# Making a state-space layer's tables and block matrices during the preceding layer's second MLP projections

## What is computed

```
dt = exp(log_dt);  mag = exp(dt * a_re)
abar = mag * (cos(dt * a_im), sin(dt * a_im))
z = (abar - 1) / a                        # complex
bbar = z * b                              # 64 groups x 64 states x 16 inputs
h_t = abar * h_{t-1} + bbar @ u_t         # per group, over 512 tokens; samples: one step
y = Re(c @ h) + d * x
out = val * sigmoid(gate),  (val, gate) = gelu(y) @ w_glu + b_glu
```

## Time and profile before

| what | value |
|---|---|
| median of 3 runs (lowest, highest) | 3161.78 us (3157.08, 3167.73) |
| the profiled execution | 3174.09 us, span 3172.3 us |
| busy: PE, DVE, ACT, POOL | 2914.1, 1476.5, 1051.6, 1048.5 us |
| instructions: PE, DVE, ACT, POOL | 22548, 2162, 1620, 548 |
| bytes read, written | 242.24 MB, 23.07 MB |

### The profile page before, as it was taken

The page is one execution under the profiler, slowest core; times in us unless marked ns, Lnnn a source line. Parts: engine busy times, 40 slices in busy tenths (PEclk is TensorE's granted clock), DMA queues, the critical chain, the costliest instruction groups (busy, mean ns, idle before and its releaser), DMA issues. The chain is left out here.

```text
span 3172.3 us, 55411 instructions
## 1 busy us (share of the span) xinstructions
PE 2914.1 (92%) x22548; PEld 2815.1 (89%) x22548; DVE 1476.5 (47%) x2162; ACT 1051.6 (33%) x1620; POOL 1048.5 (33%) x548
## 2 busy tenths in 40 slices
PE   7999799999899999999962679999999998999997
PEld 7999799999869999999962568999999998899997
DVE  4545455061328333714329954733526555372342
ACT  4554342122331333312241233422226454342222
POOL 2000164445522216544440015544440000554442
PEclk9989899999998889999985679999999999899999
DMA  4222123232344331322322012222323222122221
GB/s 141 82 69 76 36 82 99 93 92 87 105 80 140 128 113 54 95 92 92 93 73 54 27 41 80 82 92 92 93 80 100 82 76 75 61 80 93 87 92 67
DMA packets 118304, 267.56 MB, mean 84 GB/s; under 512 B 10274, under 2 KB 57890, under 8 KB 118018
## 3 DMA queue, kind: packets, MB, share of 16 engines
q1 hardware_dynamic: 56592, 206.10, 20.6%
q10 hardware_dynamic: 56434, 41.41, 4.9%
q0 software_dynamic: 5120, 17.83, 1.5%
HBM read 242.24 MB, written 23.07 MB: 84 GB/s over the span
## 5 line engine op out<-in xcount | busy, mean ns | idle before, releaser
L1527 PE MATMUL lp<-xh,wh 128*128 128x260 f32 x3712 | 1081.1, 291 | 12.3 <-POOL wl L394 4.9
L394 POOL TENSOR_TENSOR wl<-raw,wh 128x1024 fp32r<-128x1024 f32 x325 | 803.3, 2473 | 858.3 <-ACT wh L533 565.4
L1529 PE MATMUL lp<-xh,wl 128*128 128x260 f32 x3712 | 1063.7, 287 | 0.0
L1528 PE MATMUL lp<-xl,wh 128*128 128x260 f32 x3712 | 1061.5, 286 | 0.0
L1527 PEld LDWEIGHTS lp<-xh,wh 128*128 128x128 f32 x3712 | 715.8, 193 | 32.9 <-issue 20.5
L1528 PEld LDWEIGHTS lp<-xl,wh 128*128 128x128 f32 x3712 | 715.2, 193 | 0.4
L1529 PEld LDWEIGHTS lp<-xh,wl 128*128 128x128 f32 x3712 | 714.6, 193 | 0.0
L1529 PE MATMUL lp<-hh,wl 128*128 128x260 f32 x2048 | 578.6, 283 | 0.0
L1527 PE MATMUL lp<-hh,wh 128*128 128x260 f32 x2048 | 578.3, 282 | 0.0
L1528 PE MATMUL lp<-hl,wh 128*128 128x260 f32 x2048 | 576.7, 282 | 0.0
L1527 PEld LDWEIGHTS lp<-hh,wh 128*128 128x128 f32 x2048 | 385.5, 188 | 0.0
(11 more groups left out here) (344 smaller groups left out, 3654.5 us busy)
## 6 DMA issues: line engine op xcount, KB each, us to landing
raw<-in_wstream SPq DMA_DIRECT2D x389, 512.0 KB, 3.5
s<-in_s_in ACTq DMA_DIRECT2D x16, 512.0 KB, 5.6
out_hg_s<-s ACTq DMA_DIRECT2D x16, 512.0 KB, 3.3
pg<-in_kpages POOLq DMA_DIRECT2D x16, 512.0 KB, 4.7
pg<-in_vpages POOLq DMA_DIRECT2D x16, 512.0 KB, 5.3
bias_rows<-bsm ACTq DMA_DIRECT2D x1, 2560.0 KB
x<-in_xT ACTq DMA_DIRECT2D x4, 520.0 KB, 7.8
out_kT<-r ACTq DMA_DIRECT2D x1, 2080.0 KB, 7.0
```

Source lines behind the costliest of these rows:

```text
L394: pool.tensor_tensor(wl[:, s, :], raw[:, r_, :], wh[:, s, :].bitcast(F32), ALU.subtract).then_inc(w_low, 1)
L1527: pe.matmul(bank(T, half), wh[:, slot, w], hi[:, k0 + k, t], start=first, stop=False)
L1528: pe.matmul(bank(T, half), wh[:, slot, w], lo[:, k0 + k, t], start=False, stop=False)
L1529: ins = pe.matmul(bank(T, half), wl[:, slot, w], hi[:, k0 + k, t], start=False, stop=last)
```

## The change

The parameters of the state-space layer are loaded after the mixer norm of layer 1. In that layer's MLP, the second projections of half 0 take in between their tiles, on DVE, the angles, steps, small tables, a rotation table per group (`build_rot`, each from a table of 16 and one of 8 entries) and `bbar` (`build_bb`). The second projections of half 1 take the block matrices of all groups (`products`, P and Q, after one clearing of the space). ACT does the exponentials and sines there and stores every table and matrix to DRAM (8 x 512 KB rotations, 8 x 512 KB P, 8 x 640 KB Q). In the state-space layer ACT loads them back per group into two buffers each. The norm before the layer writes `xp` in place of `xh`, and POOL makes no `xl` there; the store and load of the regrouped `x` go in two parts, the first inside the norm. DVE's loop holds only `states(k)`. PE does block_kernels(0) ahead of block_inputs(0). An unused mask `keep` is gone. The diff, cut to its core:

```diff
+    def rot_built_in(k):
+        return lwf[:, 2 * N * (k % 3):2 * N * (k % 3) + D]
+    ang = lwf[:, 4 * N:4 * N + D].rearrange("p (q m t) -> p q m t", q=4, t=S5T)
+    rtemp = lwf[:, 6 * N:6 * N + D].rearrange("p (q n) -> p q n", q=2)
+    def p_built_in(k):
+        return xhf[:, D * (k % 2):D * (k % 2 + 1)]
+    def q_built_in(k):
+        return xlf[:, 5 * D // 4 * (k % 2):5 * D // 4 * (k % 2 + 1)]
...
+                    if feeds_s5(ln + 1):
+                        for a in range(3):
+                            pool.wait_ge(rot_stored[a], 16 * ((KT - 1 - a) // 3 + 1))
...
-                if not last:
+                if feeds_s5(ln):
+                    act.activation(xp[:, m], row[:, 0:NP_].rearrange("p (b j) -> p j b", j=BLK), ACT.Identity, bias=shift
+                                   ).then_inc(xp_ready, 1)
+                elif not last:
                     act.activation(xh[:, m, :], row, ACT.Identity, bias=shift).then_inc(xh_ready, 1)
                 act.activation(x[:, m, :], row, ACT.Identity, bias=shift).then_inc(x_ready, 1)
+                if feeds_s5(ln) and m == 3:
+                    regroup_out(0)
+                    p_turned(0, 0)
+                if feeds_s5(ln) and m == 5:
+                    regroup_in(0)
+                    p_turned(0, 1)
+                    for load in (load_p, load_rot, load_q):
+                        load(1)
...
+        def regroup_in(g):
+            act.wait_ge(xs_stored, 16 * (g + 1))
+            act.wait_ge(s5_zeroed, 3)
+            for j in range(BLK):
+                q = BLK - 1 - j
+                act.dma_start(xr[32 * q:32 * q + 32, 16 * g:16 * g + 16, NS:NS + NB],
+                              xs[4 * g:4 * g + 4, :, :, j, :].rearrange("k t c b -> c (k t) b")).then_inc(xr_loaded[g], 16)
+        def load_p(k):
+            act.wait_ge(pq_stored[k % 2], 32 * (k // 2 + 1))
+            if k >= 2:
+                act.wait_ge(bd_ready, k - 1)
+            act.dma_start(pn2[:, k % 2, :], p_dram[k]).then_inc(p_loaded[k % 2], 16)
+        def load_q(k):
+            act.wait_ge(pq_stored[k % 2], 32 * (k // 2 + 1))
+            act.dma_start(qn2[:, k % 2, :], q_dram[k]).then_inc(qr_loaded[k % 2], 16)
+        def load_rot(k):
+            act.wait_ge(rot_stored[k % 3], 16 * (k // 3 + 1))
+            act.dma_start(rot2[:, k % 2, :], rot_dram[k]).then_inc(qr_loaded[k % 2], 16)
+        def p_turned(k, g):
+            if k == 0:
+                act.wait_ge(p_built, 4 * KT)
+            act.wait_ge(trs_ready, 2 * k + g + 1)
+            if k and g == 0:
+                act.wait_ge(s_ready, k)
+            act.activation(ptr[:, 2 * g:2 * g + 2].rearrange("p t a s -> p (t a s)"), lp[:, 3, :], ACT.Copy
+                           ).then_inc(pt_out, 1)
+            if g == 1:
+                if k:
+                    act.wait_ge(k_ready, k)
+                act.activation(bd, pn(k)[:, :, :, 0, :], ACT.Copy).then_inc(bd_ready, 1)
...
+        def store_rot(k):
+            act.wait_ge(rot_built, k + 1)
+            act.dma_start(rot_dram[k], rot_built_in(k)).then_inc(rot_stored[k % 3], 16)
+        def ahead_of_s5(c):
+            if c == 0:
+                act.wait_ge(s5_loaded, 16 * 5)
+                act.activation(s5v[:, 2, :], s5v[:, 2, :], ACT.Exp).then_inc(s5_dt, 1)
+            if c == 1:
+                act.wait_ge(s5_arg, 1)
+                act.activation(s5v[:, 12, :], s5v[:, 3, :], ACT.Exp, scale=float(BLK)).then_inc(s5_mag, 1)
+                act.wait_ge(s5_mag, 1)
+                act.activation(s5v[:, 3, :], s5v[:, 3, :], ACT.Exp).then_inc(s5_mag, 1)
+            if c == 2:
+                act.wait_ge(s5_red, 1)
+                act.activation(ang[:, 2], ang[:, 2], ACT.Sin).then_inc(s5_sin, 1)
+                act.activation(ang[:, 3], ang[:, 3], ACT.Sin).then_inc(s5_sin, 1)
+            if c in (8, 10, 12, 14):
+                store_rot(c - 8)
+                store_rot(c - 7)
+        def ahead_of_s5_pq(m):
+            if m == 0:
+                act.wait_ge(bb_built, 1)
+                act.dma_start(s5s, I["s5_s"]).then_inc(s5_loaded, 16)
+            act.wait_ge(p_built, 4 * (m + 1))
+            act.dma_start(p_dram[m], p_built_in(m)).then_inc(pq_stored[m % 2], 16)
+            act.wait_ge(q_built, 4 * (m + 1))
+            act.dma_start(q_dram[m], q_built_in(m)).then_inc(pq_stored[m % 2], 16)
...
+                regroup_out(1)
+                xr4 = xr[:].rearrange("p (k t) n -> p k t n", t=4)
                 act.wait_ge(x_ready, 16 * y["i"])
...
+                for b in range(2):
+                    act.wait_ge(pq_stored[b], 32 * KT // 2)
                 for t in range(4):
                     f = slice(32 * t, 32 * t + 32)
                     act.activation(xr4[96:128, :, t, 0:NS], x[f, :, NP_:N], ACT.Copy).then_inc(xr_samples, 1)
                     act.activation(xr4[0:32, :, t, NS + NB:XW], x[f, :, NP_:N], ACT.Copy).then_inc(xr_samples, 1)
...
+                load_p(2)
+                p_turned(1, 0)
+                p_turned(1, 1)
+                load_p(3)
+                regroup_in(1)
...
-                turned_out(0)
-                turned_out(1)
                 for k in range(KT):
                     kernels_out(k)
                     if k >= 2:
...
                         bring_back(k - 1)
                     gelu(k)
                     if k + 2 < KT:
-                        turned_out(k + 2)
+                        load_rot(k + 2)
+                        load_q(k + 2)
+                        p_turned(k + 2, 0)
+                        p_turned(k + 2, 1)
+                    if k + 4 < KT:
+                        load_p(k + 4)
...
+                if half == 0 and feeds_s5(ln + 1):
+                    for c in range(2 * KT):
+                        high_at(c1 + c + AHEAD)
+                        ahead_of_s5(c)
...
+                        if m == 0 and feeds_s5(ln + 1):
+                            for a in range(3):
+                                act.wait_ge(rot_stored[a], 16 * ((KT - 1 - a) // 3 + 1))
                         squares(ln + 1, tile_out, t1 + m + 1, m)
+                        if feeds_s5(ln + 1):
+                            ahead_of_s5_pq(m)
+            if feeds_s5(ln + 1):
+                for load in (load_p, load_rot, load_q):
+                    load(0)
...
+        def build_rot(k):
+            if k >= 3:
+                dve.wait_ge(rot_stored[k % 3], 16 * (k // 3))
+            out = rot_built_in(k).rearrange("p (a t h l) -> p a t h l", a=2, t=4, l=8)
+            tk, shape = slice(4 * k, 4 * k + 4), [P, 4, 16, 8]
+            hi = [htab[:, a, tk].unsqueeze(3).to_broadcast(shape) for a in range(2)]
+            lo = [ltab[:, a, tk].unsqueeze(2).to_broadcast(shape) for a in range(2)]
+            tmp = [rtemp[:, q, :].rearrange("p (t h l) -> p t h l", t=4, l=8) for q in range(2)]
+            mul(out[:, 0], hi[0], lo[0])
+            mul(tmp[0], hi[1], lo[1])
+            mul(out[:, 1], hi[0], lo[1])
+            mul(tmp[1], hi[1], lo[0])
+            link.wait()
+            link.mark(dve.tensor_tensor(out[:, 0], out[:, 0], tmp[0], ALU.subtract))
+            dve.tensor_tensor(out[:, 1], out[:, 1], tmp[1], ALU.add).then_inc(rot_built, 1)
+            link.wait()
+            dve.wait_ge(rot_built, k + 1)
+        def build_bb():
+            dve.wait_ge(rot_built, KT)
+            zb_ = [a.unsqueeze(2).to_broadcast([P, S5T, 16]) for a in (zr, zi)]
+            tmp = temps(S5T, 16)
+            mul(bb_[:, 0], zb_[0], braw[:, 0])
+            mul(bb_[:, 1], zb_[0], braw[:, 1])
+            mul(tmp[0], zb_[1], braw[:, 1])
+            mul(tmp[1], zb_[1], braw[:, 0])
+            link.wait()
+            link.mark(dve.tensor_tensor(bb_[:, 0], bb_[:, 0], tmp[0], ALU.subtract))
+            dve.tensor_tensor(bb_[:, 1], bb_[:, 1], tmp[1], ALU.add).then_inc(bb_built, 1)
+            link.wait()
+            dve.wait_ge(bb_built, 1)
+            for a in range(3):
+                dve.wait_ge(rot_stored[a], 16 * ((KT - 1 - a) // 3 + 1))
+        def products(k, src, lo, n, signs, out, done):
...
+        def ahead_of_s5(half, m, c1):
+            if half == 0:
+                if m == 0:
+                    s5_angles()
+                if m == 1:
+                    s5_steps()
+                if m == 2:
+                    s5_tables()
+                if 3 <= m < 7:
+                    build_rot(2 * m - 6)
+                    build_rot(2 * m - 5)
+                if m == 7:
+                    build_bb()
+                return
+            if m == 0:
+                dve.wait_ge(chunk_done, c1)
+                link.mark(dve.memset(xhf[:, 0:2 * D], 0.0))
+                link.step(dve.memset(xlf[:, 0:5 * D // 2], 0.0))
+            if m >= 2:
+                dve.wait_ge(pq_stored[m % 2], 32 * (m // 2))
+            products(m, bb_, 0, 4, (ALU.subtract, ALU.add), p_view(p_built_in(m)), p_built)
```

(54 more changed lines are left out.)

330 lines of the change are left out of this document (142 added, 188 removed).

## The result

| | before | after |
|---|---|---|
| median of the runs | 3159.4 us | 3064.2 us (3052.3 to 3072.9) |
| after / before | | 0.9695, 95% interval 0.9664 to 0.9727 |
| profiled execution, its span | 3174.1, 3172.3 us | 3059.5, 3057.9 us |

The changed kernel is 95 us faster; 84 were forecast, 3064 lies in the range of 3043 to 3115. Two further series of it gave 3057.9 both times (ratios 0.9675 and 0.9691).

A forecast was written before the change was run, and what follows sets the result against it. PE was taken to bound the second projections, DVE's tables and builds the state-space front and loop. 3174.1 - 56.5 - 57.4 + 6 + 23 + 1 = 3090.2, or 3078 us against the median; range 3043 to 3115.

The forecast's parts named there:

- Part A: Front of the state-space layer, norm to first `states`: 32.9 us in place of 89.4, 56.5 less (bounds 52 to 59).
- the cold means: Norm after the second projections: PE, having stood up to 15 us, meets its means at 1.2 GHz, costing 1 us.
- Part B: State-space loop: without builds DVE bounds the period at 12.1 us; 100.2 in place of 157.6, 57.4 less.
- The terms of the two ends: State-space loop: first group slow, states 11.0 us, outputs and kernels 8.3; last group 8.3.
- the waits for loads: State-space loop: PE and `states` wait for loads issued about a period earlier, costing nothing.
- R2: Rival: the state-space loop stays at 1.2 GHz, 26 us more than forecast, 3104 us; chance 0.2.
- R3: Rival: ACT's order takes DVE's place in the loop, period stays near 20 us, 48 more, 3126; chance 0.06.
- Part C, second half: Second projections, half 1: DVE's matrix products, blocked by POOL, end late, costing 23 us (bounds 0 and 28).
- R1: Rival: POOL's work costs DVE nothing in the second projections, so moved work there costs 0, 3048 us; chance 0.15.
- Part C, first half: Second projections, half 0: rotations and `bbar` beside POOL end at about 104 us, costing PE 6 (bounds 0 to 10).
- the late high parts: Second projections, half 0: ACT's high parts of coming chunks, behind store_rot, are late by up to 13 us but hidden.
- R4: Rival: weight loads in the layer before fall behind 24 stores on the same DMA engines, 127 us lost, 3205; chance 0.05.

The follow-up runs named there:

- experiment 3: Changed kernel with seven further turns of the block inputs on VectorE in each group of the loop: 3125.6 us.
- experiment 4: Changed kernel with one further turn of the block inputs on VectorE in each group of the loop: loop 108.0 us instead of 94.4.
- experiment 5: Changed kernel with ScalarE copying the second half of the turned P five times instead of once in groups 2 to 7: loop 112.3 us, period 13.57.
- experiment 6: Changed kernel with one more ScalarE copy of the turned P's second half in groups 2 to 7: 146.64 us from last residual to first gated output.
- experiment 1: Changed kernel with GpSimd writing zeros twice instead of making the weights' lower parts in layer 1's second-half second projections: 3030.0 us.
- experiment 2: Changed kernel without the multiplications that make P and Q, each sum writing one row of 16: 3029.8 us.
- version 8: Changed kernel with Q(3) made before the norm, Q(4) to Q(7) behind it, GpSimd issuing their stores; computes everything: 3048.7 us against 3057.9.
- experiment 7: Changed kernel with all eight rotation stores issued at the end of the first half, VectorE not waiting for them: rotation pairs 12.67 to 14.28 us.
- version 9: Late-products kernel with three Qs spread to the second, fourth and sixth tile, zeroing in the second, ScalarE's loads later: 3038.2 us against the changed kernel's 3057.9.
- version 10: Late-products kernel with Qs in the first three tiles and the zeroing of the products' space moved from VectorE to GpSimd: 3038.4 us, ratio 0.9619 to before.

## Why the prediction was right, and where its terms were off

**Part A held, by 3.6 us too little.** From the last residual to the first turn 59.15 us less, where the prediction had 56.5, less 1 for the cold means. From ACT's first instruction of the norm to the first turn it took 28.3 us, where the terms (all but the 1.5 ahead of the norm) give 31.4. ACT's rows are slower than taken (1.73 us a row, 8 x 1.65 forecast: +0.6). The term that was mis-sized is regroup_in(0): 1.5 for the store to land and 2.8 for four issues; the store landed while ACT worked on, and the issues and their hand-over took 2.05. The copies and three loads behind it took 1.6, not 2.4, and the first half's store and the copy of turned P 0.5, not 1.05, since an issue can run beside ACT's work (that of 1654.83 beside the row's second instruction, from 1654.70). The bound of 0 for that wait was the right one.

**Part B held in its mechanism, DVE's chain at 2.4 GHz.** Experiments 3 and 4 show the chain. The size was off by 5.8 us: 94.4, not 100.2. The period is 10.78 in the steady groups, under the lower of the two bounds given, 10.9; the six periods forecast at 72.6 took 66.3. I took 12.1 with the last copy at 1.39 us; GpSimd's split falls elsewhere in the shorter period, and it takes 0.17 us in all eight groups of after. The terms of the two ends were each wrong and right in sum by luck: the second group's states came 10.8 us after the first's, not 19.3, and the last group took 17.3 to the gated projections, not 8.3: 28.1 us for 27.6. And the waits for loads weren't quite nothing, as the prediction had them:

```profile
1696.00 2.35 DVE L1613 TENSOR_TENSOR lw<-rot,mb 128x1024 f32<-128x1024 f32 x2 [0.33 <-DMA qn<-s_q]
```

In this one long period of after, 12.29 us, VectorE also waits 0.99 us for TensorE's block_kernels. R2 (1.2 GHz) falls, and so does R3: in after the block inputs, the end of ScalarE's and TensorE's chain, are done 1.0 us before VectorE wants them, and experiments 5 and 6 show what happens when they are late. What the prediction said of the clock, that DVE's builds made TensorE's pauses, is borne out by experiment 3, which puts pauses back and gets the clock down.

**Part C, second half: right, 21.8 for 23**, and by its reason: experiments 1 and 2 put the whole amount on GpSimd's reads, and R1 falls. Its sum, POOL's total beside DVE's, can be had more simply per tile: VectorE's 8.94 us of experiment 1 (residuals 1530.76 and 1539.70; the sum of squares, which still reads, is in them: four multiplications take 2.59 us beside it and 1.43 alone) and GpSimd's two subtractions at their own 2.39 (experiment 2) make 13.72, where 13.65 is measured, against 11.48 of TensorE's. A tile without Q, whose instructions take 3.6 us, comes to 10.1 by the same sum; version 8 measured 10.05.

**Part C, first half: 0.9 for 6.** The step that failed is the stretching of 38.7 us by 0.585 to 63.6, which counts 11 lower parts and nearly their full 2.4 us each. In the trace the rotations and bbar took 57.8 us (1381.06 to 1438.9). Nine lower parts ran beside them, and the instructions that they hit are 19.4 us longer than their undisturbed kind, 2.16 us for each; 57.8 - 19.4 = 38.4 is VectorE's own work, as forecast. A pair of rotations shows it: the first four multiplications meet a lower part and take 4.69 us, the second four meet none and take 2.50.

```profile
1406.58 4.69 DVE L1230 TENSOR_TENSOR lw<-bslot,ltab 128x512 f32<-128x512 f32 x4
1411.30 2.77 DVE L1322 TENSOR_TENSOR lw<-lw 128x512 f32<-128x512 f32 x1
1413.99 0.68 DVE L1323 TENSOR_TENSOR lw<-lw 128x512 f32<-128x512 f32 x1
1414.76 2.50 DVE L1230 TENSOR_TENSOR lw<-bslot,ltab 128x512 f32<-128x512 f32 x4
```

So DVE ended 97.9 us behind h, not 104: 5.5 us late, not 11, and the two PSUM pairs took that up, as the prediction says they take 5.7. That only nine ran and not ten, one in each 5.74 us, fits ScalarE's stand in store_rot, but experiment 7 shows no large effect of it. That the late high parts are hidden held.

**R4 falls.** In the two halves ScalarE waited once for a weight load, 0.9 us:

```profile
ACT wh L587 <- DMA raw<-in_wstream: 0.9, 1, 0.9
```

The landing of `raw` kept its median of 3.5 us, also between 1535 and 1640 us, beside the stores of the block matrices.

**The total.** Forecast 84 less. The profiled spans, without the 12.3, are 102 apart: 3.6 more than forecast from A (with the cold means), 5.8 from B, 5.1 from the first half, 1.2 from the second and 2.4 from the rest. All five misses went the same way, so none hid another. The medians are 95 apart, since the profiled execution of after lay 4.7 under its median and before's median came out 2.4 lower than the 3161.8 that the forecast started from. With the scatter of the loop the traces make the change worth 97 to 101 us; the three series gave 95, 104 and 97. The 5 in the sum of the range's lower end has no source in the prediction; without it the range begins at 3038, and nothing hangs on it.

## What to carry to other kernels

Work moved onto an engine that looks idle has to be priced at the engine's *shared* rate: for two-input VectorE instructions beside GpSimd reading SBUF, add GpSimd's instruction time to VectorE's own and compare the sum, over the whole stretch and per tile, with the bounding engine. If it is over, look for gaps where GpSimd is silent (here some 20 us around the norm), and give GpSimd work that only writes. And a short wait of TensorE's can cost more than its length, since the next matmuls may run at half the clock.

## What the runs showed of the hardware

- GpSimd's memsets (1.97 us for two of 1024 columns, 3.31 for 3840) leave VectorE's two-input instructions at their speed; its subtraction of 1024 columns holds them up for about 2.35, nearly its own length (2.39 alone in experiment 2, 2.5 beside them). A one-input copy of 128x8 took 1.39 us instead of 0.17 beside GpSimd's split of 128x520, in before and in experiment 4.
- TensorE stood for 3.2 us in experiment 5 and 7.6 in experiment 3 ahead of matmuls at 1.2 GHz, and for 0.69 and 1.15 us in after's steady groups ahead of matmuls at 2.4. The same 1.31 us of experiment 6 came ahead of either, and so did 3.75 us in experiment 4 (L2114 at 1714.13 in 0.63 us, at 1727.78 in 1.11), so the length of the last pause alone doesn't decide it.
- A store of 640 KB issued by GpSimd (0.53 us to issue) was reported back after 6.0 us in the median of five in version 8 (5.6 in version 9, 6.9 in version 10), where ScalarE's took 3.9.
